# Splitting the gate weights of layer 1 into rounded and residual halves, with a ring of half units

## The reference, cut to what matters

```
h = rms_norm(x, mix_norm)
u_a, q_b, f_b, i_b, og_b, cx_c, v_c, o_c, ig_c, fg_c, gates = split(h @ w_in)   # gates: 3 x 2048 columns
y_a = s5_mixer(u_a, ...)      # state-space scan, 512 wide, then gelu and a GLU with w_glu
y_b = hgrn2_mixer(q_b, f_b, i_b, og_b, ...)   # 6 heads, decayed attention
y_c = mlstm_mixer(cx_c, v_c, o_c, ig_c, fg_c, ...)  # 4 heads of 192
merged = sigmoid(g_a) * (y_a @ wb[:512]) + sigmoid(g_b) * (y_b @ wb[512:1280]) + sigmoid(g_c) * (y_c @ wb[1280:])
x = x + merged @ w_out
x = x + conv_ffn(rms_norm(x, ffn_norm), w_up, conv_w, conv_b, w_down)
```

## Time and profile before

| | |
|---|---|
| median of three executions | 3019.06 us (3014.05 to 3021.58) |
| profiled execution, its own time | 3016.22 us |
| its span in the profile | 3014.4 us |
| TensorE busy | 2988.2 us, 99% |
| VectorE busy | 1955.5 us, 65% |
| ScalarE busy | 1219.7 us, 40% |
| GpSimd busy | 69.6 us, 2% |
| granted TensorE clock, whole span | 1.00 |

### The profile page before, as it was taken

How to read it: one execution, slowest core, us unless ns; L and a number is a source line. 1 busy time by engine, 2 the same in 40 slices (tenths; PEclk the granted TensorE clock), 3 DMA queues, 4 the chain that set the end, 5 groups by cost and what they waited for, 6 DMA issues and landing times.

```text
span 3014.4 us, 45535 instructions
## 1 busy us (share of the span) xinstructions
PE 2988.2 (99%) x17784; PEld 2635.9 (87%) x17784; DVE 1955.5 (65%) x2558; ACT 1219.7 (40%) x1351; POOL 69.6 (2%) x72
## 2 busy tenths in 40 slices
PE   8999999999999999999999999999999999999999
PEld 8899888889988888888888888876998888888888
DVE  6674253785778888886557776636667666666444
ACT  5353101204444444444444344425445444444333
POOL 0000000000001000000000000000000000000000
PEclk9999999999999999999999999999999999999999
DMA  6554332445555555555555554540455555555555
GB/s 227 182 185 157 126 112 91 168 145 174 189 183 193 195 195 193 191 187 182 196 192 202 191 184 163 182 164 29 157 192 195 194 190 190 192 194 179 194 193 186
DMA packets 80146, 530.20 MB, mean 176 GB/s; under 512 B 9152, under 2 KB 9536, under 8 KB 27712
## 3 DMA queue, kind: packets, MB, share of 16 engines
q1 hardware_dynamic: 80064, 529.07, 50.6%
HBM read 526.94 MB, written 2.10 MB: 175 GB/s over the span
## 4 chain that ended last, share of the span: by engine, by line
PE 98%; DVE 1%; ACT 1%; DMA 0%; issue 0%; SPq 0%; DVEq 0%; ACTq 0%
PE bank L503 98%; DVE w_low L1550 0%; PE bank L1019 0%; ACT w_high L1078 0%; DMA xT<-in_xT 0%; DVE arena L1547 0%; DVE acts_both L1550 0%; ACT arena L1521 0%; ACT mix_high L1190 0%; ACT L1209 0%; ACT L1190 0%; ACT arena L1097 0%; ACT arena L1452 0%; ACT arena L1493 0%; DVE xtmp L1550 0%
## 5 line engine op out<-in xcount | busy, mean ns | idle before, releaser
L1550 DVE TENSOR_TENSOR w_low<-ring,w_high 128x2048 fp32r<-128x2048 f32 (+1 forms) x480 | 1014.3, 2114 | 385.7 <-ACT w_high L1078 382.0
L1078 ACT ACTIVATE w_high<-ring 128x2048 fp32r<-128x2048 f32 (+1 forms) x480 | 849.5, 1771 | 642.2 <-DMA ring<-in_w_down 223.7
L503 PE MATMUL bank<-up_early,w_high 128*128 128x512 f32 x1408 | 487.8, 389 | 0.0
L503 PE MATMUL bank<-up_late,w_high 128*128 128x512 f32 x1408 | 487.4, 389 | 0.0
L503 PE MATMUL bank<-acts_both,w_high 128*128 128x512 f32 x1408 | 479.0, 389 | 0.3 <-DVE w_low L1550 0.3
L503 PE MATMUL bank<-up_early,w_low 128*128 128x256 f32 x1408 | 388.7, 276 | 0.0
L503 PE MATMUL bank<-up_late,w_low 128*128 128x256 f32 x1408 | 388.6, 276 | 0.0
L503 PE MATMUL bank<-acts_both,w_low 128*128 128x256 f32 x1408 | 388.6, 276 | 0.0
L503 PE MATMUL bank<-hT,ring 128*128 128x256 f32 x1536 | 336.7, 380 | 0.0
L503 PEld LDWEIGHTS bank<-hT,ring 128*128 128x128 f32 x1536 | 290.2, 190 | 41.9 <-issue 3.3
L503 PEld LDWEIGHTS bank<-up_early,w_high 128*128 128x128 f32 x1408 | 264.5, 188 | 55.2
(11 more groups left out here) (284 smaller groups left out, 4193.6 us busy)
## 6 DMA issues: line engine op xcount, KB each, us to landing
ring<-in_w_up SPq DMA_DIRECT2D x176, 1024.0 KB, 4.8
ring<-in_w_down SPq DMA_DIRECT2D x128, 704.0 KB, 4.0
ring<-in_w_in SPq DMA_DIRECT2D x66, 1024.0 KB, 4.8
ring<-in_w_mix SPq DMA_DIRECT2D x62, 1024.0 KB, 4.9
ring<-in_w_gates SPq DMA_DIRECT2D x48, 1024.0 KB, 4.9
ring<-in_w_branch SPq DMA_DIRECT2D x16, 1024.0 KB, 4.9
ring<-in_w_out SPq DMA_DIRECT2D x16, 1024.0 KB, 4.8
ring<-in_w_o SPq DMA_DIRECT2D x16, 1024.0 KB, 4.9
```

Source lines behind the costliest of these rows:

```text
L503: return nc.tensor.matmul(o, lhsT, rhs, start=first, stop=last)
L1078: A(w_high[:, s, 0:cols], ring[:, s, 0:cols], ACT.Copy).then_inc(rounded[s], 1)
L1550: return V.tensor_tensor(o, a, b, op)
```

## The change

- The 48 gate units of layer 1 become split units. They stream through a second ring of half units (8 of the 16 weight tiles, 512 KB). Four raw halves lie in ring slots 0 and 1, their rounded forms in slots 2 and 3, and the residual lies over the raw half, so the ring holds two gate units.
- ScalarE rounds each half (`round_gate`), one gate unit ahead of the sigmoid. GpSimd, not VectorE, lowers it: 96 `tensor_tensor` subtractions of 128x1024 (`half_low`), after four of the same size for the activation (`h_low`). ScalarE also rounds the activation (`h_high`, four copies of 128x1024).
- Each gate unit is 48 fp32r matmuls, done in two halves; each half waits for its own lowering.
- The order of the gate units changes, each product of 2048 x 128 standing at another place than before. Gate 0 comes behind both parts of the query and key product. Gates 0 to 7 lie in the mLSTM part, 8 to 15 behind the HGRN levels, 16 to 18 around its output, 19 to 22 behind the S5 inputs, 23 to 41 during the recurrence, 42 to 47 behind the S5 output matmuls, and then the GLU product. There is no gate unit between the two parts of `w_qk`, nor behind the GLU product.
- `w_qk` is loaded as four parts into the half slots once the last units of the input projection have been consumed. `s5_b` and `s5_c` are loaded into the arena in one transfer each; the load of `s5_c`, and the load of gate 41 that stands behind it in SyncE's order, wait for the fourth turn table.
- The gate tiles are laid out by `gate_tile`, in whatever arena tiles are free at that time. The merge reads them with a stride, and sums into `out_sum`; `out_high` and `out_low`, `y_high` and `u_high` move. In layer 2, `align(1)` sets the ring to slot 1 ahead of `w_mix2`.

The core of the diff:

```diff
+GATES, HALF = 48, UNIT // 2
+GATES_FED = 42
...
+        half_raw = ring[:, 0:2].rearrange("p s (q c) -> p (s q) c", c=HALF)
+        half_low = alias("half_low", ring_base, [P, RING, HALF])
+        half_high = alias("half_high", ring_base, [P, RING, HALF], 2 * UNIT // T)
...
+            for c in range(19):
+                load_gate(c)
+            sp.wait_ge(hg_out, 1)
+            sp.dma_start(s5_b, t["s5_b"]).then_inc(s5_b_landed, 16)
+            for c in range(19, GATES_FED - 1):
+                load_gate(c)
+            sp.wait_ge(s5_tabled, S5_TILES)
+            sp.dma_start(s5_c, t["s5_c"]).then_inc(s5_c_landed, 16)
+            for c in range(GATES_FED - 1, GATES - 1):
+                load_gate(c)
...
+            def gate():
+
+                at = (halves.pos + 1) % RING
+                free = halves.drained[at].value()
+                if free > 0:
+                    pe.wait_ge(drained[at], free)
+                for half in range(2):
+                    s, _, _, _, _ = halves.next(half == 1, True)
+                    pe.wait_ge(half_lowered[s], halves.lowered[s].value())
+                    for j in range(KT // 2):
+                        k, c = KT // 2 * half + j, slice(j * P, (j + 1) * P)
+                        mm(bank[at][:, 0], half_high[:, s, c], h_high[:, k], k == 0, False)
+                        mm(bank[at][:, 0], half_high[:, s, c], h_low[:, k], False, False)
+                        last = mm(bank[at][:, 0], half_low[:, s, c], h_high[:, k], False, k == KT - 1)
+                    last.then_inc(half_consumed[s], 1)
...
-                unit(project)
-            rounds(4, project)
-            unit(project)
-            unit(project)
...
+                gate()
+            for c in range(23, GATES_FED):
+                gate()
...
+            def round_gate():
+                for half in range(2):
+                    s, there, _, _, _ = halves_ahead.next(False, split=True)
+                    act.wait_ge(half_landed[s], there)
+                    A(half_high[:, s], half_raw[:, s], ACT.Copy).then_inc(half_rounded[s], 1)
...
+            halves = Units(half_landed, half_rounded, half_lowered, half_consumed, drained)
+            halves.skip(4, False)
+            pool.wait_ge(if_summed, 1)
+            for q in range(RING):
+                pool.wait_ge(h_rounded, q + 1)
+                lower(h_low[:, 4 * q:4 * q + 4], hT[:, 4 * q:4 * q + 4], h_high[:, 4 * q:4 * q + 4])\
+                    .then_inc(h_lowered, 1)
+            for c in range(2 * GATES):
+                s, _, _, _, _ = halves.next(False, split=True)
+                pool.wait_ge(half_rounded[s], halves.rounded[s].value())
+                lower(half_low[:, s], half_raw[:, s], half_high[:, s]).then_inc(half_lowered[s], 1)
             lower_acts()
             lower_acts()
```

More of the change, by code:

```diff
@@ L98, with gate_of, gate_tile @@
 IN2, GATES2, TOKENS2 = 26, 32, 8
+GATES, HALF = 48, UNIT // 2
+GATES_FED = 42
+def gate_of(c):
+    if c < 12 or 28 <= c < 32:
+        return 0, c if c < 12 else c - 16
+    return (1, c if c < 16 else c - 16) if c < 28 else (2, c - 32)
+def gate_tile(c):
+    for first, last, at in ((0, 28, 62), (28, 30, 44), (30, 42, 4), (42, 46, 90), (46, 48, 40)):
+        if first <= c < last:
+            return at + c - first
+GATE_TILE = {gate_of(c): gate_tile(c) for c in range(GATES)}
 WHOLE2 = 3
@@ L458, in _, with load_half @@
[L458 to L464, removed]
+            halves = Units(half_landed, half_rounded, half_lowered, half_consumed, drained)
+            def load_half(src, cols=HALF, after=None):
+                s, _, before, _, _ = halves.next(False)
+                if after is None:
+                    sp.wait_ge(half_consumed[s], before)
+                else:
+                    for q in after:
+                        sp.wait_ge(consumed[q], units.consumed[q].value())
+                sp.dma_start(half_raw[:, s, 0:cols], src).then_inc(half_landed[s], 16)
@@ new lines, in _, with load_over @@
+            for half in range(2):
+                load_half(t["w_glu"][0][:, half * HALF:(half + 1) * HALF])
+            glu = [c.value() for c in halves.consumed[0:2]]
+            def load_over(src, after):
+                s, _, before, _, _ = units.next(False)
+                sp.wait_ge(consumed[s], before)
+                for q, n in after:
+                    sp.wait_ge(half_consumed[q], n)
+                sp.dma_start(ring[:, s], src).then_inc(landed[s], 16)
+            load_over(t["w_branch"][0], [(0, free[0]), (1, free[1])])
@@ L480, in _ @@
                 load(t["w_ukv"][j])
+            units.align(1)
             stream(t["w_mix2"], 4)
@@ L833, in _ @@
                             pe.wait_ge(s5_in, 4 * (f - 1) + n + 1)
-                        last = mm(bank[4 + n][:, part], ring[r, s, c:c + P], MT[r, U0 + f])
+                        last = mm(bank[4 + n][:, part], s5_b[r, c:c + P], MT[r, U0 + f])
                         if part:
-                            last.then_inc(consumed[s] if f % 2 and n == 3 else s5_fed, 1)
-                unit(project)
-            rounds(4, project)
-            unit(project)
-            unit(project)
-            s = take()
+                            last.then_inc(s5_fed, 1)
+                gate()
+            for c in range(23, GATES_FED):
+                gate()
+            pe.wait_ge(s5_c_landed, 16)
             for f in range(S5_TILES):
@@ L1512, in _ @@
             ahead.skip(units.pos - ahead.pos, False)
+            units.align(1)
+            ahead.align(1)
             for i in range(2 * HEADS):
@@ L1884, in _ @@
             dve.wait_ge(norm_done, 3)
-            for half in range(2):
-                units.skip(1, False)
-                units.skip(2)
-            skip(4)
-            units.skip(2)
             for n in range(S5_STATES):
@@ L1955, in _, with merge @@
             merges = [0]
-            def merge(g, high, low, split, whole=0):
-                base, last_bank = merges[0], g.shape[1] == 3
+            def merge(pair, third, high, low, split):
+                base = merges[0]
                 merges[0] += 1
```

276 lines of the change are left out of this document (155 added, 121 removed).

## The result

The changed kernel takes 3063.42 us, the median of four executions (3062.27 to 3070.86); the kernel before took 3019.17 in four executions on the same chip (3014.05 to 3021.58). The ratio is 1.0154, 95% interval 1.0133 to 1.0175: 44 us slower. The forecast was 3066 us, range 3012 to 3095, slower with 0.77. The profiled execution took 3062.51 us, its span is 3060.7 us.

What follows compares the result with a forecast made beforehand. TensorE was taken to bound the kernel, but GpSimd's lowerings to stretch VectorE's S5 chain: branches at 754.0 instead of 705.3 us, 49 more. 3016.2 + 49 = 3065, the runs' median 2.8 above the profiled execution: 3066 us, range 3012 to 3095.

Steps and rivals of the forecast that it cites:

- What the change removes: Layer 1's 48 gate units: 5.65 us split instead of 6.91 plain, 60.5 us less TensorE time, 2.0%.
- One half: GpSimd lowering of 128x1024: 2.30 us exclusive of VectorE, adding 2.16 us to a saturated VectorE chain (bounds 0.96 and 2.26).
- The recurrence: S5 recurrence: 38 halves lowered within VectorE's chain add 82.1 us, making it 193.9 instead of 111.8; TensorE runs dry.
- The part before it: Up to the last S5 input: 206.3 us if TensorE never waits, plus 22 us of waits (8 to 35).
- (a): Between the two query/key parts: no covering unit, so the drain and its signals are open, 1.7 us.
- (b): The two row norms: factor of 4.3 us plus 4.3 for some two lowerings, against 5.65 of cover; 3 us each.
- (c): First HGRN level: VectorE needs 17.6 us including three lowerings, TensorE has 2.7 and 5.65; 9.2 us open.
- (d): Six further HGRN levels: VectorE 9.9 us with up to two lowerings against 8.35; 5 us in all.
- (1) no blocking: Rival: GpSimd works beside VectorE, the S5 chain stays at 111.8 us, time 2968 us; chance 0.15 for 2955 to 3000.
- (3) a starved GpSimd: Rival: VectorE always gets in first, chain 111.8 us with TensorE dry, 17 units follow, 3088 us; chance 0.10.
- (2) a cheap half: Rival: a half adds only 0.96 us in the recurrence, time about 3009 us, up to 3028; chance 0.09.
- (4): Rival: clock falls during TensorE's wait of some 60 us, first unit behind takes 5.7 us more; no separate chance given.

Runs made afterwards that it cites:

- Experiments 1 and 2: Changed kernel, GpSimd lowering only 32 of 1024 columns per half: in gates 24 to 42 (1), 2984.18 us; in all other gates (2), 3050.01 us.
- experiment 3: Changed kernel, but in gates 24 to 42 three write-only GpSimd memsets replace each half's subtraction: 2985.2 us.
- experiment 4: Changed kernel, but in gates 24 to 42 GpSimd does two subtractions for each half, the second on the high half alone: 3129.15 us.
- experiment 8: Changed kernel with gates 25 to 47 plain, one gate moved behind the first HGRN level, one more plain unit in each row norm: 3003.43 us.
- experiment 5: Changed kernel, but VectorE lowers the 34 halves of gates 24 to 40, one behind every third instruction of the recurrence: 3037.89 us.
- experiments 9 to 11: Kernel of experiment 8 with 4, 16 or 64 already-satisfied TensorE waits ahead of layer 1's down projection: 2998.69, 2994.94 and 3000.35 us.

## Why the prediction was right

**What the change removes.** Partly off in size. A split gate takes 736.65 to 742.41 = 5.76 us in the changed kernel's ScalarE drains, not the 5.65 of the input units: 48 matmuls at 0.120 us each instead of 0.118. The gain on offer was 55 us and not 60.5.

**One half, the deciding term.** The mechanism and the size of the whole are right; that they agree to half a microsecond is luck. Predicted were 38 halves in the chain at 2.16 us, together 82.1. The chain grew by 194.3 - 111.8 = 82.5 us, but over 40 halves: the two of gate 23, which the prediction took to be lowered before the chain starts, fall into it as well, and the first holds up VectorE's first product (3.06 us instead of 1.23). That is 82.5 / 40 = 2.06 us a half. Experiments 1 and 2, which each count 38 halves, give 2.07 and 2.08. So a half costs 0.09 us less than predicted, 3.4 us in all, and two more of them cost 4.1. The rows of the feed-forward part, in which GpSimd's lowering ended 0.60 us behind VectorE's end wherever it began, gave the mechanism. By the prediction's own terms the exclusive time is 2.07 + 0.14 = 2.21 us and not 2.30, against 4 x 0.60 = 2.40 if all of it grew with the columns. With the wait in it a row of GpSimd is 3.2 us long on average, not 3.4 to 3.7. Experiment 1 shows that the lowerings cause the length of the recurrence, and experiment 3 that reading is what matters. The estimate of 2.35 us, worked out in the prediction from the Trainium skill, "GPSIMD Engine Reference", section 3.1, agrees with the 2.37 alone, and its 2.07 added is what was measured.

**The recurrence.** Predicted 513.6 to 707.5 us, measured 514.26 to 708.59. TensorE ran dry at 632.9 us, with a unit each 6.68 us until then (predicted 6.8) and a wait of 0.30 in each. As predicted, the queue with gate 41 in it cost nothing more.

**The part before it.** The total was right for partly wrong reasons, and so by luck: last S5 input at 509.87 us (509.4 predicted), that is 23.2 us over the ideal 206.3 where 22 were forecast. (a) 1.7 as forecast. (b) 2.0 at each norm, not 3: two lowerings fell on the row factor, as forecast, but lengthened it by 3.6 us and not by 4.3 (two of its products take 1.90 and 2.48 us instead of 0.41 each), and the unit over it is 5.76 long. (c) 7.9, not 9.2; the eight products took 13.77 us instead of 7.42, 6.35 more where three lowerings were to give 6.5. (d) Nothing at the later levels, where 5 were forecast: three `copy_predicated` and four products, with the lowerings between them, fitted under the unit; one lowering at a time held up a product there. That makes 13.6 us of waits against 22. The balance is TensorE's own time, 214.9 us busy instead of 205: 2.4 from the 5.76 of 22 units, about 5 from the clock, which the prediction had only behind the long wait, and some 2.5 us that I can't place. The clock in windows of the changed kernel (the number after the busy times): 20 us behind the query/key wait, then at the first norm, the first level and the second norm. The five stretches without a wait give 5 x (0.19 + 0.15 + 0.27 + 0.16 + 0.19) = 4.8 us:

```profile
315.00:320.00 5.00, 5.00 (x28) 4.35 (x27) 1.99 (x3) 2.99 (x5) 1.45 (x1) 0.81 0.42 135
320.00:325.00 5.00, 5.00 (x36) 4.80 (x35) 0.00 (x0) 4.90 (x8) 2.45 (x2) 0.85 0.30 103
...
370.00:375.00 5.00, 5.00 (x33) 4.91 (x33) 4.53 (x9) 0.70 (x1) 2.69 (x2) 0.73 0.00 0
390.00:395.00 5.00, 1.52 (x7) 1.55 (x8) 3.30 (x4) 0.47 (x1) 3.52 (x2) 0.50 0.00 0
395.00:400.00 5.00, 5.00 (x38) 5.00 (x38) 2.07 (x4) 0.00 (x0) 0.00 (x0) 0.84 0.00 0
...
480.00:485.00 5.00, 5.00 (x33) 4.62 (x32) 3.17 (x7) 0.15 (x1) 2.36 (x1) 0.81 0.00 0
```

**Behind the chain.** 46.5 us forecast from its end to the branches, 48.2 measured (708.6 to 756.8). TensorE is below full clock at first there (0.60 from 710 to 715 us). The rest of the kernel, forecast as unchanged, is 5.2 us shorter (2303.9 us from the branches on instead of 2309.1): 2.6 of these are the output product's pace above. So the 49 us more that were forecast stand against 51.5 up to the branches, and 46.3 in the whole span: the rest, for which no change was forecast, took 5.2 back.

**The rivals.** (1) no blocking and (3) a starved GpSimd are refuted by the turns that the two timelines show. (2) a cheap half by the 2.07 us added. (4) The clock did fall to its lower level in the long wait (0.50 from 640 to 690 us). The first unit behind it took 7.4 us, 1.7 more than a split gate and not 5.7, and TensorE waits another 8.3 us for VectorE's chain behind it, so it cost nothing there; the clock cost more where it wasn't looked for.

**The change as a whole.** By experiment, the interference in the recurrence costs 79 us (1) and that in the front 13 (2). The gain in TensorE time is real; kernel 1, which does as many matmuls but leaves most of the lowering of 19 gates out, ran 1.1% faster than before.

## What to carry to other kernels

Before work is given to an idle GpSimd, look at what VectorE does beside it: if VectorE is on a chain of instructions with two SBUF operands that another engine's work merely covers, each GpSimd instruction that reads SBUF is added to the chain at nearly its full length, and here that was 2.07 us of 2.37 where VectorE would have needed at most 1.20. Count which of them fall into the chain from its first instruction on, and measure one of the same kind, since another subtraction cost 1.58 (experiment 4). A faster matmul form for filler work gives nothing where the filler covers a chain of another engine; use it where TensorE sets the time and keep the slow form, which needs no lowering, for the cover. And when units get shorter, count again at every place at which one unit was just long enough.

## What the runs showed of the hardware that I had not expected

- A granted clock below full with TensorE busy: 0.73 from 370 to 375 us, a wholly busy stretch behind a wait of 2.0 us, and 0.81 and 0.85 in two wholly busy stretches from 315 to 325 us. There the last wait, of 1.7 us, lies 20 us back, and 8 short matmuls with 4 partitions (2.0 us) stand at the start. From 318.3 to 321.2 us matmuls of 256 columns follow each other every 0.213 us instead of 0.120. The kernel before has waits of up to 1.1 us in this stage and 1.00 throughout. Filling the two norms' waits took the mean from 360 to 400 us from 0.90 to 0.99 (experiment 8). But experiment 5 has the same wait of 2.0 us at the first norm and 1.00 from 365 to 380 us, so what brings the clock down isn't shown. The Trainium skill, "TensorE: Matmul & The Clock Gate", Part 1, calls the slow clock the default that activity releases; the rows agree for the long wait, with 0.50 in it and 1.00 later, and don't settle the short ones.
- A write-only GpSimd instruction leaves VectorE alone (experiment 3).
- A second GpSimd subtraction right behind the first, with one tile as both operands, cost VectorE's chain 1.58 us and not 2.07 (experiment 4). Not explained.
- Pairs of matmuls of 512 and 256 columns run at 340 or 350 ns through a whole product at full clock with no wait, differently for the same product in different kernels. Not explained (experiments 9 to 11).
